# Running totals of decays by matrix products, a norm's squares moved ahead of split pieces, and three weight units taken from GpSimd

## The reference, cut to what matters

```python
u = rmsnorm(h, norm_w)
z, xbc, dt_raw, q, k, v, g_ssd, g_att = split_cols(u @ w_in, IN_WIDTHS)
dt = softplus(dt_raw + dt_bias)
a = -exp(a_log)                       # 32 heads
cs = cumsum(dt * a, axis=time)        # the running totals of the decays
lmat = exp(where(causal, cs[l] - cs[s], -inf))
y_diag = einsum(cb, lmat, x * dt)
```

## Time and profile before

| | before |
|---|---|
| median of 3 runs | 1708.4 us (1703.85 to 1708.52) |
| the profiled execution, its own time | 1711.74 us |
| its span | 1709.9 us |
| PE busy | 1638.2 us, 96% |
| DVE busy | 1124.0 us, 66% |
| ACT busy | 929.0 us, 54% |
| POOL busy | 219.9 us, 13% |
| HBM read | 262.89 MB, 154 GB/s over the span |

### The profile page before, as it was taken

The page is one execution under the profiler, slowest core; times in us unless marked ns, Lnnn a source line. Parts: engine busy times, 40 slices in busy tenths (PEclk is TensorE's granted clock), DMA queues, the critical chain, the costliest instruction groups (busy, mean ns, idle before and its releaser), DMA issues.

```text
span 1709.9 us, 31740 instructions
## 1 busy us (share of the span) xinstructions
PE 1638.2 (96%) x12831; PEld 1581.1 (92%) x12831; DVE 1124.0 (66%) x2457; ACT 929.0 (54%) x2014; POOL 219.9 (13%) x224
## 2 busy tenths in 40 slices
PE   7999999999999999999899999799999888999998
PEld 7999989999999899999899998688898778999997
DVE  5555588787647876564487756844457877678862
ACT  5444364564436654365565544556575666466652
POOL 5000000000000000001100001144432662100000
PEclk9999999999999999999999999899999999999999
DMA  8555545555555555643355556433354224545551
GB/s 264 173 173 163 183 148 173 164 171 173 164 177 167 174 173 167 187 141 124 124 169 177 177 182 194 133 99 99 99 173 124 77 90 132 173 154 191 168 182 46
DMA packets 260210, 266.03 MB, mean 156 GB/s; under 512 B 4755, under 2 KB 259025, under 8 KB 260064
## 3 DMA queue, kind: packets, MB, share of 16 engines
q1 hardware_dynamic: 258528, 260.72, 48.3%
q0 software_dynamic: 1536, 3.28, 0.8%
HBM read 262.89 MB, written 1.09 MB: 154 GB/s over the span
## 4 chain that ended last, share of the span: by engine, by line
PE 87%; DVE 6%; ACT 4%; issue 2%; DMA 0%; POOL 0%; SPq 0%; DVEq 0%; ACTq 0%; POOLq 0%
PE ps L904 53%; PE ps L906 26%; DVE wl L2029 1%; ACT wh L1375 1%; DVE CY L2116 1%; PE ps L682 1%; DVE CY L1997 0%; PE ps L683 0%; PE ps L671 0%; DMA X<-in_x 0%; ACT swP L1117 0%; PE ps L748 0%; DVE SY L2002 0%; ACT EX L1323 0%; PE ps L615 0%
## 5 line engine op out<-in xcount | busy, mean ns | idle before, releaser
L2029 DVE TENSOR_TENSOR wl<-raw,wh 128x512 fp32r<-128x512 f32 x925 | 609.1, 707 | 308.6 <-ACT wh L1375 301.6
L1375 ACT ACTIVATE wh<-raw 128x512 fp32r<-128x512 f32 (+1 forms) x989 | 552.1, 618 | 207.1 <-PE ps L904 206.6
L904 PE MATMUL ps<-XH,wh 128*128 128x258 f32 (+3 forms) x2528 | 646.6, 291 | 10.6 <-ACT XH L1003 4.7
L906 PE MATMUL ps<-XH,wl 128*128 128x258 f32 (+3 forms) x2528 | 637.1, 287 | 0.0
L904 PEld LDWEIGHTS ps<-XH,wh 128*128 128x128 f32 x2528 | 483.0, 191 | 19.0 <-issue 11.8
L906 PEld LDWEIGHTS ps<-XH,wl 128*128 128x128 f32 x2528 | 482.5, 191 | 0.3
L904 PE MATMUL ps<-XL,wh 128*128 128x258 f32 (+3 forms) x2528 | 350.1, 288 | 0.0
L904 PEld LDWEIGHTS ps<-XL,wh 128*128 128x128 f32 x2528 | 326.0, 190 | 3.3 <-issue 2.4
L906 PE MATMUL ps<-HH,wl 128*128 128x272 f32 (+1 forms) x704 | 172.9, 283 | 0.0
L904 PE MATMUL ps<-HH,wh 128*128 128x272 f32 (+1 forms) x704 | 172.9, 284 | 0.0
L906 PEld LDWEIGHTS ps<-HH,wl 128*128 128x128 f32 x704 | 132.4, 188 | 0.0
(11 more groups left out here) (424 smaller groups left out, 2140.7 us busy)
## 6 DMA issues: line engine op xcount, KB each, us to landing
raw<-in_ffn_wg SPq DMA_DIRECT2D x44, 1024.0 KB, 5.3
raw<-in_ffn_wu SPq DMA_DIRECT2D x44, 1024.0 KB, 5.4
raw<-in_w_in SPq DMA_DIRECT2D x33, 1024.0 KB, 5.3
raw<-in_ffn_wd SPq DMA_DIRECT2D x32, 1024.0 KB, 5.2
raw<-in_w_ffn_in SPq DMA_DIRECT2D x22, 1024.0 KB, 5.1
raw<-in_ffn_wd SPq DMA_DIRECT2D x16, 768.0 KB, 4.7
raw<-in_conv_w_in SPq DMA_DIRECT2D x12, 1024.0 KB, 5.1
raw<-in_kv_w SPq DMA_DIRECT2D x8, 1024.0 KB, 5.3
```

The costliest lines, as they stand in the source:

```text
L904: mm = e.matmul(o, hi[:, k, c], xk, start=u.first and part == 0 and k == 0, stop=u.last and end)
L906: e.matmul(o, lo[:, k, c], xk, start=False, stop=False)
L1375: e.activation(wh[u.n % NH][:, c], raw[u.n % NR][:, c], ACT.Copy).then_inc(s_hi, 1)
L2029: e.tensor_tensor(wl[u.n % NR][:, c], raw[u.n % NR][:, c], wh[u.n % NH][:, c].bitcast(F32), ALU.subtract).then_inc(s_lo, 1)
```

## The change

1. **Squares.** The four squares (ACT) and four additions (DVE) move from side steps of their own into the last step of `act_norm5` and `dve_norm5`, so they stand ahead of the split pieces of the groups `kv2` and `dt`. The third square goes to a new tile SQB. The groups `kv2` and `dt` have no side steps beside them; PE's sum of squares (L776) is one step behind `dt`.
2. **Running totals.** The two CSB buffers and the nine additions go. PE transposes dt alone; ACT copies it to DTT; DVE multiplies the transposed dt by -exp(a_log), which is now loaded on all 128 partitions, into a new tile DTA; nine PE products with the triangle `tri` give the totals in both layouts, CST and DCP, in PSUM bank 6. CSH, CSL, NCT, PCT and BD are made from these. Behind `q2` stand 13 side steps instead of 20, at rate 3.6 instead of 6.
3. **GpSimd.** The units z 0, 1 and 2 give POOL no pieces; DVE makes all four of each.

The diff, cut to its core:

```diff
+    with ExitStack() as st:
+        SQB = sb(st, "SQB", [128, 2, T])
...
-        CSB = [sb(st, f"CSB{i}", [128, 256 + T]) for i in range(2)]
-    DC_ = CSB[1][:, 256:256 + T]
+        DTA = sb(st, "DTA", [128, 3, 128])
+    CST, DCP = PS[6][:, 96:192], PS[6][:, 192:192 + T]
...
-    P.queue(1 + 7)
+    P.queue(1)
     P.run("ln5", 1)
-    P.rate, P.credit = 4, 0.01
     P.group("kv2", W_IN, KD, K0, 2, two(s_cr, 24))
     P.group("dt", W_IN, KD, DT0, 1, [(s_cr, 27)])
+    P.queue(1)
     P.drain("rs6")
-    P.queue(20)
-    P.rate, P.credit = 6, 0.0
+    P.queue(13)
+    P.rate, P.credit = 3.6, 0.0
...
-    P.rate, P.pool = 9, (1, 3)
+    P.rate = 9
     for j in range(8):
+        P.pool = (1, 3) if j > 2 else ()
         P.group(("z", j), W_IN, KD, Z0 + 256 * j, 2, two(s_z2, 2 * j))
...
@@ pe_steps
-        yield from idle(3 + 3 + 9 + 1)
+        yield from idle(4)
         e.wait_ge(s_dt, 1)
-        e.wait_ge(s_cum2, 10)
         e.wait_ge(s_vm, 18)
         for i, (t0, t1) in enumerate(ST):
-            e.transpose(PS[6][0:t1 - t0, 32 * i:32 * i + 32], ZD[:, t0:t1], ident[0:32, 0:32])
-            tr = e.transpose(PS[6][0:t1 - t0, 96 + 32 * i:128 + 32 * i], DC_[0:32, t0:t1], ident[0:32, 0:32])
+            tr = e.transpose(PS[6][0:t1 - t0, 32 * i:32 * i + 32], ZD[:, t0:t1], ident[0:32, 0:32])
         tr.then_inc(s_dT, 1)
+        yield
+        yield
+        e.wait_ge(s_cum2, 2)
+        e.wait_ge(s_c, 32)
+        e.matmul(CST[:, 0:32], tri[:, 0:128], DTA[:, 0, 0:32], start=True, stop=True)
+        e.matmul(CST[:, 32:64], tri[:, 128:256], DTA[:, 0, 0:32], start=True, stop=False)
+        e.matmul(CST[:, 32:64], tri[:, 272:400], DTA[:, 1, 0:32], start=False, stop=True)
+        e.matmul(CST[0:16, 64:96], tri[:, 256:272], DTA[:, 0, 0:32], start=True, stop=False)
+        e.matmul(CST[0:16, 64:96], tri[:, 400:416], DTA[:, 1, 0:32], start=False, stop=False)
+        e.matmul(CST[0:16, 64:96], tri[0:16, 416:432], DTA[0:16, 2, 0:32], start=False, stop=True)
+        e.matmul(DCP[:, 0:T], DTA[:, 0, :], tri[:, 0:T], start=True, stop=False)
+        e.matmul(DCP[:, 128:T], DTA[:, 1, :], tri[:, 272:416], start=False, stop=False)
+        e.matmul(DCP[:, 256:T], DTA[0:16, 2, :], tri[0:16, 416:432], start=False, stop=True).then_inc(s_dT, 1)
+        yield
+        yield
+        yield
         e.wait_ge(s_bd, 1)
...
@@ act_norm5, behind UH
+        for j, q in enumerate((SQ[:, 0:2, :], SQ[:, 2:4, :], SQB[:], SQ[:, 2:4, :])):
+            e.wait_ge(s_h, 40 + 2 * j + 2)
+            if j == 3:
+                e.wait_ge(s_qa, 17)
+            e.activation(q, H[:, 2 * j:2 * j + 2, :], ACT.Square).then_inc(s_sq2, 1)
...
@@ act_dt
+        e.wait_ge(s_dT, 2)
+        e.activation(CSH[:], DCP, ACT.Copy).then_inc(s_csh, 1)
+        e.activation(NCT[:, 0:2, :], src3(CST[:, 0:64], 2), ACT.Copy, scale=-1.0).then_inc(s_dtt, 1)
+        e.activation(NCT[0:16, 2, :], CST[0:16, 64:96], ACT.Copy, scale=-1.0).then_inc(s_dtt, 1)
+        e.activation(PCT[:, 0:2, :], src3(CST[:, 0:64], 2), ACT.Copy).then_inc(s_dtt, 1)
...
@@ dve_norm5, behind UL
+        for n, q in enumerate((SQ[:, 2:4, :], SQB[:], SQ[:, 2:4, :])):
+            e.wait_ge(s_sq2, n + 2)
+            if n:
+                e.wait_ge(s_qa, 16 + n)
+            e.tensor_tensor(SQ[:, 0:2, :], SQ[:, 0:2, :], q, ALU.add).then_inc(s_qa, 1)
...
@@ dve_dt
-        e.tensor_scalar(CSB[0][0:32, 256:256 + T], ZD[:], AN[:, 0:1], None, ALU.mult).then_inc(s_cum2, 1)
-        yield
-        yield from dve_cumsum(e, CSB, 32, s_cum2)
+        e.wait_ge(s_dtt, 2)
+        e.tensor_tensor(DTA[:, 0:2, 0:32], src3(PS[6][:, 0:64], 2), AN[:].unsqueeze(1).to_broadcast([128, 2, 32]),
+                        ALU.mult).then_inc(s_cum2, 1)
+        e.tensor_tensor(DTA[0:16, 2, 0:32], PS[6][0:16, 64:96], AN[0:16, :], ALU.mult).then_inc(s_cum2, 1)
+        yield
+        yield
+        yield
+        e.wait_ge(s_dtt, 5)
```

More of the change, by code:

```diff
@@ L279, in build @@
     DTT, NCT, PCT = (sb(ma, n, [128, 3, 32]) for n in ("DTT", "NCT", "PCT"))
-    DTB, AN, DC, DC2 = sb(ma, "DTB", [32, 1]), sb(ma, "AN", [32, 1]), sb(ma, "DC", [128, 16]), sb(ma, "DC2", [128, 32])
+    DTB, AN, DC, DC2 = sb(ma, "DTB", [32, 1]), sb(ma, "AN", [128, 32]), sb(ma, "DC", [128, 16]), sb(ma, "DC2", [128, 32])
     EX2 = sb(ma, "E16", [16, 512])
@@ L773, in pe_steps @@
         yield from pe_norm5(e)
-        yield from idle(5)
         e.wait_ge(s_qa, 20)
         e.matmul(PS[6][:, 0:T], mean1[:], SQ[:, 0, 0:T], start=True, stop=True).then_inc(s_sum, 1)
-        yield
         yield
@@ L783, in pe_steps @@
         yield
-        yield from idle(3 + 3 + 9 + 1)
+        yield from idle(4)
         e.wait_ge(s_dt, 1)
-        e.wait_ge(s_cum2, 10)
         e.wait_ge(s_vm, 18)
         for i, (t0, t1) in enumerate(ST):
-            e.transpose(PS[6][0:t1 - t0, 32 * i:32 * i + 32], ZD[:, t0:t1], ident[0:32, 0:32])
-            tr = e.transpose(PS[6][0:t1 - t0, 96 + 32 * i:128 + 32 * i], DC_[0:32, t0:t1], ident[0:32, 0:32])
+            tr = e.transpose(PS[6][0:t1 - t0, 32 * i:32 * i + 32], ZD[:, t0:t1], ident[0:32, 0:32])
         tr.then_inc(s_dT, 1)
+        yield
[14 more added lines that the diff above has]
+        yield
         e.wait_ge(s_bd, 1)
-        e.wait_ge(s_c, 32)
         e.matmul(PS[7][0:16, :], tri[0:32, 128:144], BD[:], start=True, stop=True).then_inc(s_b2, 1)
@@ L1283, in act_dt @@
         yield from act_softplus(e, ZD[:], 32, LD[:], s_sp2)
-        yield
         e.activation(AN[:], AN[:], ACT.Exp).then_inc(s_na, 1)
         yield
-        yield from idle(1 + 9)
-        e.wait_ge(s_cum2, 10)
-        e.activation(CSH[:], DC_, ACT.Copy).then_inc(s_csh, 1)
         yield
         e.wait_ge(s_dT, 1)
[L1292 to L1295, removed]
+        e.activation(DTT[:, 0:2, :], src3(PS[6][:, 0:64], 2), ACT.Copy, scale=0.5).then_inc(s_dtt, 1)
+        e.activation(DTT[0:16, 2, :], PS[6][0:16, 64:96], ACT.Copy, scale=0.5).then_inc(s_dtt, 1)
+        yield
[6 more added lines that the diff above has]
+        yield
+        yield
         yield
@@ L1682, in dve_norm5 @@
         e.memset(sw.PT0[:], 0.0).then_inc(s_kz0, 1)
-        for b in CSB:
-            e.memset(b[:], 0.0).then_inc(s_csz, 1)
+        e.memset(DTA[:], 0.0).then_inc(s_csz, 1)
         e.wait_ge(s_rs, 6)
@@ L1711, in dve_mix_sum @@
         yield
-        yield from idle(2)
     def dve_mix_chunk(e, i):
@@ L1881, in dve_steps @@
         yield from dve_norm5(e)
-        yield from dve_mix_sum(e)
+        yield
         yield from woven(dve_dt(e), lambda i: dve_mix_chunk(e, i))
@@ L1888, in dve_dt @@
     def dve_dt(e):
-        yield
-        yield from idle(3)
+        yield from idle(4)
         e.wait_ge(s_sp2, 4)
         e.scalar_tensor_tensor(out=ZD[:], in0=ZD[:], scalar=0.0, in1=LD[:], op0=ALU.max, op1=ALU.add).then_inc(s_dt, 1)
-        yield
         e.wait_ge(s_na, 1)
@@ L1896, in dve_dt @@
         yield
-        e.wait_ge(s_dt, 1)
+        yield
+        e.wait_ge(s_dtt, 2)
         e.wait_ge(s_nega, 1)
-        e.wait_ge(s_csz, 2)
-        e.tensor_scalar(CSB[0][0:32, 256:256 + T], ZD[:], AN[:, 0:1], None, ALU.mult).then_inc(s_cum2, 1)
+        e.wait_ge(s_csz, 1)
+        e.tensor_tensor(DTA[:, 0:2, 0:32], src3(PS[6][:, 0:64], 2), AN[:].unsqueeze(1).to_broadcast([128, 2, 32]),
+                        ALU.mult).then_inc(s_cum2, 1)
+        e.tensor_tensor(DTA[0:16, 2, 0:32], PS[6][0:16, 64:96], AN[0:16, :], ALU.mult).then_inc(s_cum2, 1)
         yield
-        yield from dve_cumsum(e, CSB, 32, s_cum2)
-        e.wait_ge(s_cum2, 10)
-        e.tensor_tensor(BD[:].rearrange("p (h t) -> p h t", h=32), DC_[0:32, 256:T].unsqueeze(1).to_broadcast([32, 32, 16]),
+        yield
+        yield
+        e.wait_ge(s_dtt, 5)
+        e.tensor_tensor(BD[:].rearrange("p (h t) -> p h t", h=32), DCP[0:32, 256:T].unsqueeze(1).to_broadcast([32, 32, 16]),
                         ident[0:32, 0:32].unsqueeze(2).to_broadcast([32, 32, 16]), ALU.mult).then_inc(s_bd, 1)
         e.wait_ge(s_csh, 1)
-        e.tensor_tensor(CSL[:], DC_, CSH[:].bitcast(F32), ALU.subtract).then_inc(s_csl, 1)
+        e.tensor_tensor(CSL[:], DCP, CSH[:].bitcast(F32), ALU.subtract).then_inc(s_csl, 1)
         yield
@@ L2346, in pool_steps @@
             yield from idle(2 * (0 <= h - 2 < 8) + (h < 8))
-        yield from idle(19 + 1 + 7 + 20)
+        yield from idle(19 + 1 + 1 + 13)
         for h in range(19):
@@ L2475, in pool @@
         e.dma_start(DTB[:], A["ssd_dt_bias_2"].rearrange("l p -> p l")).then_inc(s_d, 16)
-        e.dma_start(AN[:], A["ssd_a_log_2"].rearrange("l p -> p l")).then_inc(s_d, 16)
+        al = A["ssd_a_log_2"]
+        e.dma_start(AN[:], bass.AP(tensor=al.tensor, offset=al.offset, ap=[[0, 128], [1, 32]])).then_inc(s_d, 16)
         e.dma_start(DC2[:], bass.AP(tensor=dd.tensor, offset=dd.offset, ap=[[0, 128], [1, 32]])).then_inc(s_d, 16)
```

## The result

Five runs of each kernel gave 1700.43 us (1699.27 to 1701.66) against 1706.54 us (1703.85 to 1708.52): a ratio of 0.9963, with a 95% interval from 0.9948 to 0.9977, so about 6 us less; the interval leaves out 1. The forecast was 1699.7.

The account below looks back on a forecast made before the run. TensorE (PE) was taken as the bound, losing time to two waits and low clock. New wait, q2 groups, low clock, products and BD put z 0 at 1108.5 against 1117.2, 8.7 us less: 1708.4 to 1699.7, range 1695 to 1706.

Parts of the forecast that it names:

- What bounds the kernel: Whole kernel: PE holds 87% of the chain; time is gained only at its waits (6.24 and 4.80 us) and low clock.
- given back later: Rival, attention heads beside z and ga: PE waits there for most of what it saved; gain 1.4, 1707 us; chance 0.10.
- Part 1: Squares to q2 0: the 6.24 us wait goes; a new 4.3 us wait before q2 0 ends on DVE's VV.
- The low clock: Behind the new wait before q2 0: a 3.84 us spell at low clock, a loss of 1.9 us, bounds 0 and 3.7.
- DVE's lead at DTA: At the first DTA product: DVE is 1.2 us ahead, so PE does not wait; the BD hand-off is hidden by 0.6.
- the wait moves to the totals: Rival, first DTA product: DVE late by 5, PE waits 4 plus 1.9 of low clock; gain 2.8, 1705.6; chance 0.17.
- The products: Added PE work for the totals: nine products cost 1.8 us (large ones 0.94, small ones 0.84); BD 0.9 at full clock.
- Slower, because DVE's 1.5 us are not GpSimd's: Rival, q2 0 to the DTA product: DVE instructions take 1.1 us more, PE waits 18; 1719.6 us; chance 0.06.
- The port and not the additions: Rival, running totals: GpSimd's 4.3 us excess was nearly the whole 4.80 us wait, products needless; gain 6.9, 1701.5; chance 0.07.
- The time: Whole kernel: z 0 begins 8.7 us earlier and the shift reaches the end; median 1699.7 us from 1708.4; chance 0.60.

Follow-up runs that it names:

- e6: Changed kernel with the root, QR7 and VV put ahead of the split pieces of group dt on ACT and DVE: 1697.04 us, ratio to before 0.9943.
- e0: The changed kernel as it is, run and profiled again for comparison: 1699.52 us, ratio to before 0.9959.
- r7: Changed kernel with e6's order, and GpSimd given its pieces of z 0 to 2 again: 1696.74 us, ratio to before 0.9942.
- e1: Kernel before with only the GpSimd change (no POOL pieces in z 0 to 2): 1705.46 us, ratio 0.9993.
- e3: Changed kernel with GpSimd given its two pieces of z 0 to 2 again: 1699.28 us, ratio to before 0.9958.
- e2: Kernel before with only the squares and their additions moved, nine additions of totals kept: 1702.43 us, ratio 0.9976.
- e4: Kernel before with the squares moved and no GpSimd pieces in z 0 to 2, nine additions kept: 1698.81 us, ratio 0.9955.
- r9: Changed kernel with the move of the squares undone, products kept and no GpSimd pieces in z 0 to 2: 1702.83 us, ratio to before 0.9974.
- r8: e4 with e6's order, so root first and the nine additions kept instead of the products: 1701.33 us, ratio to before 0.9964.

## Why the prediction was right, point by point

*What bounds the kernel.* Right: time came from PE's two waits and the low clock behind them, and it reached the end. From z 0 to the end of the span the kernel before took 592.7 and 589.4 us in its two profiles and the changed one 591.1 and 590.6, where the rival "given back later" asked for some 7 us more. That rival is out.

*Part 1.* Right to the tenth. Counted from kv2's first product, q2 0 was forecast at 15.8 us (1079.2 less 1063.39) and began at 15.85 (1077.24 less 1061.39); before, it was 19.56. The wait was 4.36 for 4.3, and it ended on DVE behind eight pieces, as e6 shows by taking four away. By naming these pieces the forecast already pointed at time that the change left unused.

*The low clock.* Right that it comes; the spell was 4.86 us in the first profile and 3.40 in e0 for the 3.84 that I took, so the loss was 2.4 and 1.7 us, around my 1.9.

*DVE's lead at DTA.* Forecast 1.2 us; DVE ended DTA at 1092.3 and PE came at 1093.89, a lead of 1.6. BD was ready at 1099.1 and PE came at 1101.36, a lead of 2.3 for the forecast 0.6. No wait there in any of the seven profiles with products. The rival "the wait moves to the totals" is out for the changed kernel; only e6 and r7, with q2 0 earlier, wait at the transposes (0.8 and 1.2 us).

*The products.* This term was undersized: 1.8 forecast, 2.28 measured. The six small ones took 1.06 (0.84 forecast), the three large ones 1.22 (0.94): the last, with 16 columns, took 0.32 and not 0.14. A likely reason is that its stationary side has 128 columns and not the 16 of the row that I priced it by; no run shows this by itself. BD took 0.96 for 0.9. That is 0.5 of the 0.7 us by which the stretch of 45.8 (e0) is longer than the forecast 45.1 (1108.5 less 1063.39).

*Slower, because DVE's 1.5 us are not GpSimd's.* Out: none in e0 and e1, two in e3, three in r7, four in e2 and before. None stands in any profile without POOL's pieces in q2, though in the changed kernel the DMA share there was 0.40. The Trainium skill's page "SBUF — State Buffer", section "Who interferes with whom", says that a DVE instruction with two SBUF inputs and a GpSimd instruction that reads SBUF contend for a port pair that works as an exclusive lock. These runs agree: in e3 an instruction that takes 0.42 us in the changed kernel began 0.06 us behind a piece of 1.31 and took 1.53.

*The port and not the additions.* Half right. e1 refutes that the port was the whole wait. The other half of it, that the products are PE time for nothing, is nearly true in this change: e4 does without them in the same time. The step of mine that failed is the unwritten one that each part is worth what its wait was. Part 1 gives 2.2 us of stretch at the end of the row (r9 to e0) and 3.2 alone; part 2 gives 4.8 beside part 1 (e2 to e3), 3.2 beside part 3 (e1 to r9) and 1.1 beside both (e4 to e0); part 3 gives 2.6 alone, 3.7 beside part 1 and 0 beside parts 1 and 2. Parts 2 and 3 remove the same wait. PE had less to wait for in e4 than in e1 (1.9 against 2.6 us in all). Its way from q2 0 to the transposes, the wait left out, is 18.7 us in e1 and 20.1 in e4. The likely reason is that the spell of low clock falls on q2 0 in e4 and ahead of it in e1, and so lets DVE catch up; this was not tried by itself.

*The time.* The gain was forecast at 8.7 us and measured at 6.1 and 7.4 (medians), with 8.0 in e0's stretch. The forecast of 1699.7 started from a median of three, 1708.4, that lay 1.9 above the median of five. The two errors have opposite signs, so that the forecast came within 0.7 us of 1700.4 is in part luck; the waits, their places and what ended them are not.

## What to carry to other kernels

When a stall is removed, name at once what the waiting engine meets next, and count what stands in the other engines' queues ahead of that write: here four weight pieces moved behind two short instructions gave another 2.5 us for no work at all. Two edits aimed at one wait are not to be added; run each beside the other before paying for both, and remember that an idle wait that vanished may have hidden the price of the other (in the changed kernel the products are worth 1.1 us of the stretch and nothing that the time shows, behind the earlier start of e6 3.3 us of it and some 4 of the time). Compare stretches between two fixed instructions and not spans, where executions drift by up to 3 us before the place of the change (kv2 begins at 1060.3 to 1063.4 us in the thirteen profiles).

## What the runs showed of the hardware that I had not expected

Whether PE falls to 1.2 GHz after a wait is not fixed by the length of the wait alone. After 3.9 to 6.2 us it fell in every profile. After 1.9 us before q2 0 it did not in e6 and r7, but did in r8, with the same wait (1.95), the clock from 1075 on:

```profile
1075.00:1079.00 4.00, 4.00 (x22) 3.91 (x21) 2.27 (x6) 3.85 (x11) 0.00 (x0) 0.57 0.46 154
```

And the wait of 2.2 us ahead of kv2, which every kernel has, brought a spell in two of thirteen profiles (the first of the changed kernel, and r8); neither made q2 0 later (15.85 us behind kv2's first product against 15.84 in e0, 13.44 in r8 against 13.43 in e6). So e6's one profile without a spell doesn't show that e6 never has one. In e4 even waits of 1.2 and 0.7 us in a row of short products were followed by one:

```profile
1100.40:1104.80 4.40, 4.40 (x26) 4.40 (x25) 2.61 (x5) 2.30 (x4) 0.00 (x0) 0.61 0.13 45
```
